# Forty zero products on TensorE, in one wait and around the first scores of a decoder step

## The reference

```
def compress_blocks(kv, pe, w1, w2):          # prompt and cache, blocks of 64 rows
    blocks = kv.reshape(B, L // BLK, BLK, N_KV, 2, HEAD_DIM) + pe[:, None]
    hid = jax.nn.gelu(jnp.einsum('bnlgcd,cldh->bngch', blocks, w1))
    return jnp.einsum('bngch,chd->bngcd', hid, w2)

def cmp_attend(q, pos_q, comp, slopes):       # scores against compressed keys
    s = jnp.einsum('btgpd,bngd->btgpn', q, comp[..., 0, :]) * SCALE
    s = s - slopes * dist
    p = masked_softmax(s, dist >= 0)
    return jnp.einsum('btgpn,bngd->btgpd', p, comp[..., 1, :]), p

def nsa_heads(q, pos_q, comp, gather_sel, kv_win, pos_win, gates, slopes):
    o_c, p_c = cmp_attend(q, pos_q, comp, slopes)
    idx = select_blocks(jnp.sum(p_c, axis=3), pos_q, comp.shape[1])
    o_s = slc_attend(q, pos_q, gather_sel(idx), idx, slopes)
    o_w = win_attend(q, pos_q, kv_win, pos_win, slopes)
    return gates[0] * o_c + gates[1] * o_s + gates[2] * o_w

def merge_and_mlp(x, o, pool_out, w_out, g_mlp, w_up, w_down):
    h = x + concatenate([o, pool_out]) @ w_out
    a = square(relu(rms_norm(h, g_mlp) @ w_up))
    return h + a @ w_down
```

## Time and profile before

| | us |
|---|---|
| median of 3 runs | 920.68 |
| lowest and highest | 920.35, 921.46 |
| the profiled execution, whole | 919.6 |
| its span, first to last instruction | 917.8 |
| TensorE busy in the span | 839.3 (91%) |
| VectorE, ScalarE, GpSimd busy | 442.2, 337.2, 130.9 |
| granted TensorE clock, mean of the span | 0.955 |

### The profile page before, as it was taken

One profiled execution on the slowest core, in us unless ns is written; L12 is line 12 of the kernel. 1 busy time (PEld: TensorE's weight loads), 2 busy tenths in 40 slices (PEclk: granted clock), 3 DMA queues, 4 the chain that ended last, 5 costly groups with the idle time before them and its releaser, 6 DMA issues.

```text
span 917.8 us, 17058 instructions
## 1 busy us (share of the span) xinstructions
PE 839.3 (91%) x7087; PEld 758.1 (83%) x7087; DVE 442.2 (48%) x991; ACT 337.2 (37%) x618; POOL 130.9 (14%) x125
## 2 busy tenths in 40 slices
PE   5999998887778779987999999999999999999995
PEld 4999977764445555655999999999999999999995
DVE  5435556666677566664426442334323343243432
ACT  6501055552455474553325431134212331033311
POOL 0001101201674425430120000000000000000120
PEclk8999999996898879889999999999999999999998
DMA  8912639822460013438220222222211222222002
GB/s 289 322 67 93 192 105 278 259 88 91 144 197 29 9 74 147 162 151 207 93 92 1 92 92 92 91 91 91 75 44 64 91 91 91 91 93 91 1 1 104
DMA packets 48788, 102.81 MB, mean 112 GB/s; under 512 B 7499, under 2 KB 19167, under 8 KB 46430
## 3 DMA queue, kind: packets, MB, share of 16 engines
q1 hardware_dynamic: 41821, 68.48, 22.8%
q0 software_dynamic: 6912, 33.56, 10.8%
HBM read 97.62 MB, written 8.53 MB: 116 GB/s over the span
## 4 chain that ended last, share of the span: by engine, by line
PE 51%; DVE 1%; ACT 0%; DVEq 0%; issue 0%
PE bank L2005 50%; PE bank L2046 0%; DVE y L1995 0%; PE bank L2072 0%; DVE wl L1925 0%; PE bank L2062 0%; ACT wh L1869 0%; DVE hT L1938 0%; DVE hT L1963 0%; DVE xl L1942 0%; ACT low L1883 0%; DVE xl L1931 0%; ACT xh L1885 0%; DVEq L1818 0%; ACT small L1913 0%
## 5 line engine op out<-in xcount | busy, mean ns | idle before, releaser
L2005 PE MATMUL bank<-xh,wh 128*128 128x288 f32 x640 | 138.1, 298 | 4.3 <-DVE xl L1931 3.9
L2005 PE MATMUL bank<-xl,wh 128*128 128x288 f32 x640 | 137.9, 297 | 0.0
L2005 PE MATMUL bank<-xh,wl 128*128 128x288 f32 x640 | 137.8, 297 | 0.0
L1869 ACT ACTIVATE wh<-low 128x1024 fp32r<-128x1024 f32 x72 | 75.0, 1050 | 103.1 <-PE bank L2005 102.8
L2005 PE MATMUL bank<-ah,wh 128*128 128x288 f32 x512 | 110.2, 297 | 0.0
L2005 PE MATMUL bank<-ah,wl 128*128 128x288 f32 x512 | 109.6, 296 | 0.0
L2005 PE MATMUL bank<-al,wh 128*128 128x288 f32 x512 | 109.6, 296 | 0.0
L2005 PEld LDWEIGHTS bank<-xh,wh 128*128 128x128 f32 x640 | 104.0, 190 | 4.9 <-DVE wl L1925 4.1
L2005 PEld LDWEIGHTS bank<-xl,wh 128*128 128x128 f32 x640 | 103.9, 190 | 0.0
L2005 PEld LDWEIGHTS bank<-xh,wl 128*128 128x128 f32 x640 | 103.8, 190 | 0.0
L1963 DVE TENSOR_TENSOR hT<-bank,hT 128x288 f32<-128x288 f32 x64 | 26.3, 453 | 138.8 <-PE bank L2005 138.8
(11 more groups left out here) (332 smaller groups left out, 1414.3 us busy)
## 6 DMA issues: line engine op xcount, KB each, us to landing
low<-in_w_up SPq DMA_DIRECT2D x8, 2048.0 KB, 7.8
low<-in_w_down SPq DMA_DIRECT2D x8, 2048.0 KB, 7.9
zone<-in_cmp_w SPq DMA_DIRECT2D x16, 256.0 KB
o_swin<-in_state_win SPq DMA_DIRECT2D x8, 504.0 KB
px<-in_x_prompt SPq DMA_DIRECT2D x4, 512.0 KB, 5.3
u_raw<-in_w_in SPq DMA_DIRECT2D x1, 2048.0 KB, 10.1
q_raw<-in_w_in SPq DMA_DIRECT2D x1, 2048.0 KB, 10.5
low<-in_state_win SPq DMA_DIRECT2D x4, 512.0 KB
```

Source lines behind the costliest of these rows:

```text
L1869: act.activation(wcols(m.wh, i), raw_cols(i), ACT.Copy).then_inc(wh_ready, 1)
L2005: last = pe.matmul(out(i, hf), w[wi], half(x[:, k, :], hf), start=first and part == 0, stop=end and part == 2)
```

## The change

A new helper issues products of one row of zeros with 512 columns of zeros, in bf16, into a bank that nobody reads at that time. It is called three times: 20 products between the last hidden product and the wait for the gelu, 12 ahead of the first scores of the prompt, and 8 between the second scores and the compressed scores. No wait is added or removed, and nothing is changed on the other engines.

```diff
+def busy(pe, m, bank, count):
+
+    for _ in range(count):
+        pe.matmul(bank[:, :], m.zeros[0:1, 0:P], m.zeros[0:1, P:640], start=True, stop=True)
+
@@ compress, on_tensor
                 last.then_inc(phid, 1)
 
+        busy(pe, m, pb[4], 20)
         pe.wait_ge(gelu, 5)
         pe.wait_ge(sems.w2_in, 16)
         for g in range(2):
@@ prompt, tensor
+            busy(pe, m, pb[4], 12)
             scores(0, 0)
             scores(0, 1)
+            busy(pe, m, pb[4], 8)
             pe.wait_ge(kc_ready, 1)
             for i in range(PTILES):
                 for j in range(HPG):
```

## The result

The changed kernel takes 927.26 us (median of 8 runs, 924.67 to 932.78) against 921.07 for the kernel before in the same comparison (8 runs, 917.21 to 925.41). The ratio is 1.0081, 95% interval 1.0048 to 1.0113: slower by 7.5 us (4.4 to 10.4). The forecast was 922.3 with a range to 925.5. The profiled execution took 926.36 us, its span 924.5. The mean clock of the span is 0.953 after and 0.955 before, so the mean hardly tells them apart.

What follows compares the result with a forecast made beforehand. TensorE was taken to bound much of the path, slowed by half-clock stretches around the compression and prompt. Terms -1.9 + 1.77 + 1.76 + 0 = +1.6 us gave 921.2 profiled, 922.3 as median; range 918.6 to 925.5.

Steps and rivals of the forecast that it cites:

- the first saving: Compression: 20 zeros in the gelu's wait hold the clock, so the second weights run at twice the pace; 1.9 us saved.
- the 0.22 taken for the 12 and the 8: Around the prompt's first scores: each zero product of 512 columns costs 0.22 us; ends 0.115 and 0.43 (1.2 GHz).
- a fall before 211: Sign of being wrong: the clock falls before 211, though forecast at 1.00 from 203.7 to the second weights' end.
- Second weights: End of the compression: at 2.4 GHz the last copies end at 211.9 against 213.82; -1.9 us.
- 12 products: Ahead of the prompt's first scores: only 0.87 us lies in a wait, so the scores start 1.77 us later.
- 8 products: Ahead of L1358, the compressed scores: no wait covers them, 8 x 0.22 = 1.76 us lost.
- L1358: Compressed scores: already at full clock before, so the zeros win nothing there; 0 in the sum.
- rival B: The clock falls in the middle of L1358, doubling half its 3.86 us: +1.9, to 924.2; chance 0.13.
- rival A: The zeros don't hold the clock; second weights, scores and L1358 run slow: near +11, 932; chance 0.11.
- an argument from columns: Against rival A: the zeros have 512 columns like the scores and L1035's products, under which the clock stayed at 1.00.
- Rival D: Zeros overlap or stream at twice the pace, 0.115 us each: sum -0.5, 920.2; chance 0.07.
- The ±1.5 for the later stretches at half clock: Allowance on 922.3 for seven half-clock stretches between 275.01 and 438.84 shifting; the three earlier runs lie within 1.1 us.

Runs made afterwards that it cites:

- the run with 24 and 16: Products of 128 rows of zeros, with 24 and 16 around the first scores in place of 12 and 8; ratio 1.0051 to the kernel before.
- the first run of 288 products: Kernel before plus 288 zero products in the gelu's wait, 48 each of 1, 128, 1, 64, 1, 32 rows; 1029.24 us (one run).
- the 128-row run: Changed kernel with the same 20, 12 and 8 products, each of 128 rows of zeros in place of one; ratio 0.9999 to before, 921.72 us.

## Why the prediction was wrong, point by point

**The step that failed** is the condition under the first saving, "If the zeros hold the clock at 2.4 GHz", and with it the 0.22 taken for the 12 and the 8, a full-clock price. The zeros of the change use one row of the array and do not hold the clock: it fell at 209.20, and a fall before 211 was one of the prediction's own signs of being wrong. Measured by the table, against the terms of the sum:

- Second weights: -1.9 forecast, -0.7 measured. The clock fell when they began and came up in the middle.
- 12 products: +1.77 forecast, +3.18 measured. About half of them ran at half clock.
- 8 products: +1.76 forecast, +3.79 measured from the first to the compressed scores. Here the 8 themselves were mostly at full clock (2.06 us); the rest is the first scores at half clock, 3.79 us for 1.99.
- L1358: 0 forecast, +1.55 measured. The clock fell at 226.26, in its middle, which is what rival B described, but as a part of rival A.

Sum of the stretch: +1.6 forecast, +7.8 measured.

**Rival A was the right one,** and I gave it 0.11. Its price of +11 was too high, since I had the clock down from the first scores to the end of L1358, while in this execution it rose again at 222.85, at their end. (Its five terms add up to 11.7.) In the run with only the 12 and the 8 it was down for longer still: its stretch is 10.6 us longer than before.

**What I had in hand.** The one row that spoke for A was cited and outweighed by an argument from columns: the zeros have 512 of them, as the scores and the products at L1035 have. But no stretch of the trace before showed a run of one-row products, so nothing bounded the clock under them; L996 shows two, in between other work. And the scores and L1035 differ from the zeros in the very thing that decides, and the rows had it: their records have 64 rows each and start in pairs (the two of L1035 are one row of the timeline in rows 4; those of L1303 start 0.007 us apart), one on each half of the array, so all 128 rows are in use. The honest treatment of "the trace does not show it" was two cases of like weight, and a range up to 932.

The Trainium skill, TensorE: Matmul & The Clock Gate, Part 1, has the clock follow how busy TensorE has been. This case's traces don't agree as far as busy means time: 4.15 of 4.15 us busy and the clock fell (the window 205.05:209.20 above). The measurement decides.

**What was right.** With the condition made true (128 rows) the working of the stretch held: 0.216 us per product against 0.22, the gelu's wait as full cover, -1.92 us at the second weights against -1.9, +1.86 for the 12 against +1.77, +1.73 for the 8 against +1.76, VectorE's list behind L1358 unchanged. The compressed scores, which the sum had at 0, came 0.21 us sooner, since they now ran at full clock to their end. In all it is +1.44 against +1.6. Rival D, zeros at twice the pace, is out: 20 more cost 4.32 us. The Trainium skill, TensorE: Matmul & The Clock Gate, section "Back-to-back issue gap", has 0.216 us for an isolated product, and the run with 24 and 16 agrees (4.32 us for 20 more); no run here shows its sustained 0.131, in rows of up to 288 products.

**The range.** I took the three runs shown (920.35 to 921.46) as the spread of the kernel before. Twenty-five runs of it in a later comparison went from 918.04 to 926.12. The ±1.5 for the later stretches at half clock was too narrow for single runs.

What stays open: why 64 rows of bf16 hold a clock and don't raise one, whether products of varied data would do so, and whether single rows count or blocks of them (1 and 32 rows did alike). None of this is needed for the cause of the loss.

## What to carry to other kernels

Filler products that are to keep TensorE's clock up should fill the array's rows: here 128 rows raised and held it, 64 and 96 held one that was up, one row and 32 rows did neither, and a granted clock at the first real product behind them is the check. Put them only in waits, and with room for their price at half clock (0.43 us for 512 columns), since a group that just fits at full clock overruns when it begins at half clock (3.81 us in a hole of 3.2). Where a forecast rests on the clock staying up, look for a stretch of the same kind of product in the trace; if there is none, it is an open case and not an argument.

## What the runs showed of the hardware that I had not expected

- In the first run of 288 products the clock fell twice under one-row products without any idle time of TensorE, and stayed down for 77 us of unbroken products of 1, 32 and 64 rows.
- The result of 64 rows depends on the state before: 0.50 stayed 0.50 over 20.6 us, 1.00 stayed 1.00 over 10.1 us.
- The same instructions ahead of the change ended at times from 202.61 to 209.21 us in the profiled executions (the end of the last hidden product). Stretches at half clock there come and go from one execution to the next. This one, in the compression of the 128-row run, has no counterpart in the kernel before:

```profile
175.21:182.00 6.79, 5.65 (x49) 4.86 (x51) 3.67 (x8) 3.69 (x9) 0.00 (x0) 0.50 0.96 314
```

So a difference of two profiled spans by some microseconds says nothing by itself in this kernel. The piece-by-piece table says where it is, for one execution of each, and a ratio over many runs says how much.
